# Delta rule in a hybrid decoder trunk: the order of work between the last projection and the chunk loop

## The reference

```python
p = h @ w_in                                   # q, k, v, z and two gates
qkv, z, b_pre, a_pre = split(p)
conv = silu(sum_j ext[:, j:j+L] * conv_w[j])   # four taps over time
new_conv = ext[:, L:]                          # an output: the last rows
q, k, v = split(conv); q, k = l2_normalize(q) * GD_DK**-0.5, l2_normalize(k)
def step(S, chunk):                            # one chunk, per head
    decay = exp(gam[t] - gam[s]) for s <= t
    a_mat = strict_lower(beta * (k @ k.T) * decay) + I
    u = solve(a_mat, beta * v)
    w = solve(a_mat, beta * exp(gam) * k)
    u = u - w @ S
    o = (q * exp(gam)) @ S + ((q @ k.T) * decay) @ u
    S = exp(g_last) * S + (k * exp(g_last - gam)).T @ u
o = head_rms(o) * silu(z)
y = o @ w_out
```

## Time and profile before

| | us |
|---|---|
| median of 3 runs | 2780.66 (2773.72 to 2782.38) |
| profiled execution, its own time | 2781.01 |
| its span in the profile | 2779.5 |
| PE busy | 2699.7 (97% of the span) |
| DVE busy | 1301.7 (47%) |
| ACT busy | 894.0 (32%) |
| POOL busy | 196.2 (7%) |
| chain that ended last | PE 86%, DVE 6%, ACT 3%, issue 3%, DMA 1%, POOL 1% |

### The profile page before, as it was taken

One profiled execution on the slowest core, in us unless ns is written; L12 is line 12 of the kernel. 1 busy time (PEld: TensorE's weight loads), 2 busy tenths in 40 slices (PEclk: granted clock), 3 DMA queues, 4 the chain that ended last, 5 costly groups with the idle time before them and its releaser, 6 DMA issues.

```text
span 2779.5 us, 49878 instructions
## 1 busy us (share of the span) xinstructions
PE 2699.7 (97%) x21474; PEld 2591.4 (93%) x21474; DVE 1301.7 (47%) x2086; ACT 894.0 (32%) x1127; POOL 196.2 (7%) x171
## 2 busy tenths in 40 slices
PE   7999999999989999999999999999899989999999
PEld 7999999887876999999999999999797977999998
DVE  5444334335484444433444423678435673444422
ACT  4333222134233333322222222443424342333322
POOL 2000000011010100000000000001221000100000
PEclk9999999999999999999999999999999999999999
DMA  4333324222484233332233332223215582333331
GB/s 124 91 91 102 94 77 121 54 77 68 124 270 147 77 94 94 93 105 79 81 92 91 105 94 75 63 69 90 62 43 144 170 267 87 91 91 91 105 94 52
DMA packets 476867, 280.69 MB, mean 101 GB/s; under 512 B 24940, under 2 KB 465005, under 8 KB 476707
## 3 DMA queue, kind: packets, MB, share of 16 engines
q1 hardware_dynamic: 449720, 230.83, 29.4%
q0 software_dynamic: 8704, 33.56, 3.3%
q10 hardware_dynamic: 18314, 14.45, 1.6%
HBM read 261.31 MB, written 17.69 MB: 100 GB/s over the span
## 4 chain that ended last, share of the span: by engine, by line
PE 86%; DVE 6%; issue 3%; ACT 3%; DMA 1%; POOL 1%; ACTq 0%; SPq 0%; DVEq 0%; POOLq 0%
PE ACC L436 24%; PE ACC L437 24%; PE ACC L438 24%; PE ACC L1133 2%; PE M L2219 1%; DVE w_lo L531 1%; DMA raw<-in_xa_w_k 1%; ACT w_hi L525 1%; PE ACC L2219 1%; DVE cache L1234 1%; PE M L1487 1%; DVE w_lo L546 1%; PE M L2381 1%; PE M L1562 1%; PE M L1516 1%
## 5 line engine op out<-in xcount | busy, mean ns | idle before, releaser
L436 PE MATMUL ACC<-xg_hi,w_hi 128*128 128x260 f32 x3968 | 1130.2, 285 | 11.3 <-DVE w_lo L907 7.6
L437 PE MATMUL ACC<-xg_lo,w_hi 128*128 128x260 f32 x3968 | 1124.2, 283 | 0.0
L438 PE MATMUL ACC<-xg_hi,w_lo 128*128 128x260 f32 x3968 | 1123.6, 283 | 0.0
L531 DVE TENSOR_TENSOR w_lo<-raw,w_hi 128x1024 fp32r<-128x1024 f32 (+1 forms) x326 | 421.9, 1294 | 975.9 <-ACT w_hi L525 975.6
L436 PEld LDWEIGHTS ACC<-xg_hi,w_hi 128*128 128x128 f32 x3968 | 750.5, 189 | 13.1 <-issue 8.5
L437 PEld LDWEIGHTS ACC<-xg_lo,w_hi 128*128 128x128 f32 x3968 | 751.1, 189 | 0.0
L438 PEld LDWEIGHTS ACC<-xg_hi,w_lo 128*128 128x128 f32 x3968 | 751.1, 189 | 0.0
L525 ACT ACTIVATE w_hi<-raw 128x1024 fp32r<-128x1024 f32 (+1 forms) x326 | 363.4, 1115 | 1161.8 <-PE ACC L438 1143.6
L437 PE MATMUL ACC<-hid_lo,w_hi 128*128 128x260 f32 x1408 | 399.3, 284 | 0.0
L436 PE MATMUL ACC<-hid_hi,w_hi 128*128 128x260 f32 x1408 | 398.2, 283 | 0.0
L438 PE MATMUL ACC<-hid_hi,w_lo 128*128 128x260 f32 x1408 | 398.0, 283 | 0.0
(11 more groups left out here) (556 smaller groups left out, 3262.1 us busy)
## 6 DMA issues: line engine op xcount, KB each, us to landing
raw<-in_ffn_w_gate SPq DMA_DIRECT2D x88, 512.0 KB, 3.8
raw<-in_ffn_w_up SPq DMA_DIRECT2D x88, 512.0 KB, 3.8
raw<-in_ffn_w_down SPq DMA_DIRECT2D x64, 704.0 KB, 4.6
cache<-in_cache_mem_k POOLq DMA_DIRECT2D x16, 1024.0 KB, 8.8
cache<-in_cache_mem_v POOLq DMA_DIRECT2D x16, 1024.0 KB, 8.2
raw<-in_gd_w_in SPq DMA_DIRECT2D x32, 512.0 KB, 4.2
raw<-in_ml_w_in SPq DMA_DIRECT2D x24, 512.0 KB, 3.9
raw<-in_xa_w_q SPq DMA_DIRECT2D x16, 512.0 KB, 4.4
```

Of the source, the lines that this page charges most:

```text
L436: pe.matmul(out, wh, hi[:, k0 + k, m], start=begin, stop=False)
L437: pe.matmul(out, wh, lo[:, k0 + k, m], start=False, stop=False)
L438: mm = pe.matmul(out, wl, hi[:, k0 + k, m], start=False, stop=end)
L531: dve.tensor_tensor(w_lo[:, j % 2, 0:n], raw[:, (j + d) % 4, 0:n], w_hi[:, j % 2, 0:n].bitcast(F32), ALU.subtract).then_inc(w_split, 1)
```

## The change

Six edits, all around the entry of the chunk loop:

1. The last four rounds of `substitute` and `turned` move from the end of DVE's step 7 (after the low part and the taking out of the sums) to its start.
2. `scr_w` and `scr_x` get semaphores of their own. The four transfers of chunk 0 into `XTs` start when `scr_w` has landed; POOL clears `Xs` and SP fills it when `scr_x` has. So for chunk 0 `XTs` goes first, and for the others `Xs` as before.
3. y5 waits for `Xs` alone, x5 for `XTs`. DVE's `keys(0)` waits for `scr_w` and for `turned`, no longer for `scr_x`.
4. The memory to memory copy of old convolution rows (`out_s_conv`) moves from behind the write of `scr_x` to behind the eight transfers of chunk 0.
5. ACT copies the sample keys (`sample_rows`, k8t) in step 6 of `GD_Z` rather than step 7, and applies Silu to z after `values(0)` and `conv_rows` rather than ahead of them.
6. PE waits for DVE to take out the last sums only ahead of `conv_rows`, not ahead of `values(0)` and `keys(0)`.

```diff
@@ names of ACT's events
-                       + ["z", ("v", 0)] + [("cv", n) for n in range(3)] + [(s, 0, g) for s in ("Y5", "Y6") for g in G2]
+                       + [("v", 0)] + [("cv", n) for n in range(3)] + ["z"] + [(s, 0, g) for s in ("Y5", "Y6") for g in G2]
@@ SP
-                sp.dma_start(scr_x.rearrange("c h b i j -> (c h b) i j"), blk[:]).then_inc(gd_wst, 16)
-                sp.dma_start(o["s_conv"][:, 0:2, :], a["state_gdn_conv"][0][:, 1:3, :]).then_inc(gd_st, 16)
-                sp.wait_ge(gd_wst, 32)
+                sp.dma_start(scr_x.rearrange("c h b i j -> (c h b) i j"), blk[:]).then_inc(gd_xst, 16)
+
+                def blocks(to, src, c, done):
+                    for b in range(4):
+                        r = slice(32 * b, 32 * b + 32)
+                        sp.dma_start(to[r, :, r], src[c, :, b].rearrange("h i j -> i h j")).then_inc(done, 16)
 
                 def spread(c):
                     if c == 0:
+                        sp.wait_ge(gd_wst, 16)
+                        gd_pool.wait(sp, "zt")
+                        blocks(XTs, scr_w, c, gd_xt)
+                        sp.wait_ge(gd_xst, 16)
                         gd_pool.wait(sp, "zx")
+                        blocks(Xs, scr_x, c, gd_xs)
                     else:
                         gd_dve.wait(sp, "XT5", c - 1, 1)
-                    for to, src in ((Xs, scr_x), (XTs, scr_w)):
-                        for b in range(4):
-                            r = slice(32 * b, 32 * b + 32)
-                            sp.dma_start(to[r, :, r], src[c, :, b].rearrange("h i j -> i h j")).then_inc(gd_xs, 16)
+                        blocks(Xs, scr_x, c, gd_xs)
+                        blocks(XTs, scr_w, c, gd_xt)
                 spread(0)
+                sp.dma_start(o["s_conv"][:, 0:2, :], a["state_gdn_conv"][0][:, 1:3, :]).then_inc(gd_st, 16)
                 spread(1)
@@ PE
-                    pe.wait_ge(gd_xs, 16 * 8 * (n + 1))
+                    pe.wait_ge(gd_xs, 16 * 4 * (n + 1))
                     each("y5", n, C, lambda h: rr5[:, h, :], lambda h: Xs[:, h, :])
 
                 def x5(n):
+                    pe.wait_ge(gd_xt, 16 * 4 * (n + 1))
@@ PE, entry
-                pe.wait_ge(acc_free, GD_Z.t0 + GD_Z.units)
                 gd_dve.wait(pe, "qkS")
                 gd_act.wait(pe, "k8")
                 values(0)
                 keys(0)
+                pe.wait_ge(acc_free, GD_Z.t0 + GD_Z.units)
                 conv_rows()
@@ ACT, work in the steps of GD_Z
-                z = {0: lambda: conv_silu(act, 23), 1: sample_conv, 4: sample_norms, 7: sample_rows}
+                z = {0: lambda: conv_silu(act, 23), 1: sample_conv, 4: sample_norms, 6: sample_rows}
@@ ACT, entry
+                gd_act.wait(act, "kd")
+                act.wait_ge(mm_done, GD_Z.u0 + GD_Z.units)
+                values(0)
+                conv_rows()
                 act.wait_ge(acc_free, GD_Z.t0 + GD_Z.units)
                 for n in range(4):
                     z = gp[:, 24 + 2 * n:26 + 2 * n, :]
                     ins = act.activation(z, z, ACT.Silu)
                 gd_act.done(ins, "z")
-                gd_act.wait(act, "kd")
-                values(0)
-                conv_rows()
@@ DVE, work in the steps of GD_Z
-                     5: lambda: (sample_scaled(), substitute(18, 22)), 6: lambda: (sample_dots(), substitute(22, 27)),
-                     7: lambda: (substitute(27, 31), turned())}
-                return k, q, v, z
+                     5: lambda: (sample_scaled(), substitute(18, 22)), 6: lambda: (sample_dots(), substitute(22, 27))}
+                last = {7: lambda: (substitute(27, 31), turned())}
+                return k, q, v, z, last
@@ DVE, entry
-                dve.wait_ge(gd_wst, 32)
+                dve.wait_ge(gd_wst, 16)
+                gd_dve.wait(dve, "WT")
                 keys(0)
@@ POOL
-                pool.wait_ge(gd_wst, 32)
+                pool.wait_ge(gd_xst, 16)
                 gd_pool.done(pool.memset(Xs[:], 0.0), "zx")
@@ DVE, the phase
-            dve_phase(dve, own, GD_Z, after=z)
+            dve_phase(dve, own, GD_Z, after=z, first=last)
```

More of the change, by code:

```diff
@@ L1987, in program @@
         gd_xs = sem("gd_xs")
+        gd_xt = sem("gd_xt")
+        gd_xst = sem("gd_xst")
         gd_ps = sem("gd_ps")
@@ L3137, in _ @@
                 dve_phase(dve, own, ph)
-            k, q, v, z = GDX.dve_prepare(dve, own)
+            k, q, v, z, last = GDX.dve_prepare(dve, own)
             dve_phase(dve, own, GD_K, after=k)
```

## The result

| | before | after |
|---|---|---|
| median | 2779.85 us (14 runs) | 2785.36 us (14 runs) |
| ratio, with its 95% interval | | 1.0023 (1.0014 to 1.0031) |
| the same kernel in two later sets | | 1.0015 (1.0004 to 1.0025), 1.0011 (1.0000 to 1.0021) |
| profiled execution | 2781.01 | 2788.14 |
| last unit of z to the start of xt5 of chunk 0 | 22.57 | 24.38 |

The forecast was 2779.3, a gain of 1.7. The change loses: about 2 us at the entry of the chunk loop, where all its edits are, and 3 to 6.5 us in the times. Three sets of the kernel before against itself gave 1.0000, 0.9999 and 0.9988 (the last with an interval of 0.9976 to 0.9999, which leaves out 1), so one set can be off by 0.1% and more. The lengths at the entry, read from profiles, are much firmer: 24.35, 24.69, 24.28 and 24.45 to y6 in four profiles of the kernel before, 26.38, 26.26 and 26.59 in three of the changed one.

A forecast was written before the change was run, and what follows sets the result against it. PE, busy 97% of the span, was taken as the bound, with gain only where it waits at the chunk loop's entry. y5 3.80 us earlier, limited by ACT and the clock to 1.7, gave 2781.01 to 2779.3; range 2774 to 2784.

The forecast's parts named there:

- The shares, the gaps and the chain into y5: PE busy 97%; entry gaps of 3.15, 3.41 and 5.05 us, the last ended by scr_x's write, clearing and eight transfers.
- Edits 1 to 3: At the chunk loop's entry, y5 starts 3.80 us earlier: 1.91 from the earlier rounds, 1.89 from four fewer issues ahead.
- The wait moves from the transfers to ACT: At the entry, the Silus moved behind the convolution issues are late by some 2 us, holding Yb's copy until 1974.53.
- x5 is what decides: y5 has slack behind it; x5 waits for ACT's Yb and starts at 1975.18, 2.53 us earlier.
- ACT's order (edit 5): At the entry, cvA at 1965.05, cvC at 1967.18, issues done at 1969.38, then 5.15 us of table load and Silus.
- rival B: PE's 4.2 us idle lowers the clock before conv_rows; y6 2.3 us slower, total 2783.3 us; chance 0.20.
- its own sign of being wrong: Last unit of z to xt5 (22.6 us) shorter by over 4 us or longer by over 2.5.
- the other sign: Granted clock at 0.5 from before conv_rows at the entry, which would mean the slower case of 2783.3 us.
- the values of x5 and xt5: Gain by where the clock returns: 3.40 with x5 full, 1.66 with x5 low, -0.1 with xt5 low too.
- The rule on transposes: Transposes do not count as busy like matmuls, so the entry would be cold before conv_rows; the prediction's trace spoke against it.
- The edit that I priced at nothing, edit 4: Moving out_s_conv: between minus 0.8 and plus 0.8 us on y5's start, taken as nothing because y5 has slack.
- within 0.3%: Whole kernel: median indistinguishable from no change, within about 0.3% or 8.3 us; chance 0.92.

The follow-up runs named there:

- e10: The changed kernel with the copy out_s_conv issued behind scr_x again, as before the change; 2781.71 us, ratio 1.0012.
- e1: The changed kernel with three of ACT's four Silus of z moved early into steps 5 and 6 of phase z; 2779.59 us, ratio 0.9998.
- e6: The changed kernel with ACT's four Silus back ahead of values(0) and the convolution rows; 2779.06 us, ratio 1.0004.
- before_again: The kernel before, unaltered, profiled a second time; y6 came 24.3 to 24.7 us behind the last unit, as in all four of its profiles.
- before_third: The kernel before, unaltered, profiled a third time; y6 came 24.3 to 24.7 us behind the last unit, as in all four of its profiles.
- e3: The changed kernel plus 40 useless transposes on PE in the gap ahead of the convolution rows; 2780.16 us, ratio 0.9996.
- e9: e7 plus 38 useless transposes on PE between the last convolution copy and y5; 2775.98 us, ratio 0.9994.
- e5: The kernel before with edit 1 alone (last rounds and turn ahead of the low part and sums); 2775.03 us, ratio 0.9989.
- e8: The kernel before with edits 1 and 5 only (last rounds early; sample keys in step 6, Silus behind convolution rows); 2782.99 us, ratio 1.0014.
- e2: The changed kernel with edit 1 undone, so DVE takes out the last sums ahead of the last rounds and turn; 2778.87 us, ratio 0.9994.
- after_again: The changed kernel, unaltered, with a second profile and set of times; 2784.20 us, ratio 1.0015.
- e4: The changed kernel with edit 1 undone and three Silus moved early into steps 5 and 6; 2776.56 us, ratio 0.9986.
- e7: The changed kernel with Silus early, last sums taken out between last round and turn, first convolution row not waiting for them; 2774.23 us, ratio 0.9988.

## Why the prediction was wrong

- The shares, the gaps and the chain into y5 were read rightly. Edits 1 to 3 did what they were to do: y5 started 11.5 behind the last unit, forecast 12.6. That is 1.0 better, of which 0.8 is the quicker landing of scr_x; the copy's move can be 0.2 of that (e10), the rest of it is open.
- "The wait moves from the transfers to ACT" was right, and so was that x5 is what decides. The forecast put Yb's copy at 16.7; it came at 20.1.
- **The step that failed is the start of the convolution rows in "ACT's order (edit 5)".** I priced the 24 transposes at the full clock (cvC at 9.4) although my own sum had PE idle for 4.2 us ahead of them, where it had been 3.15. That case stood as rival B, with chance 0.20, and it is what happens, in three profiles of three, and in e1, e6 and e10, which have the same gap of 4.4. I held against it that the clock had stayed full with PE idle from 1964.60 to 1968.00. One profile showed one way through the entry; before_again and before_third show the other one for the same kernel, with a gap of only 3.14 and 3.15. Of B's price, cvC at 11.6 was right (measured 11.4). That its y6 at 26.7 is so near (measured 26.3 to 26.6) is luck: it had Yb's copy at 19.0 (20.1 to 20.5), without the stalled issue, and in return xt5 at the low clock throughout (3.54), which took 1.95 to 2.17.
- By the length that the prediction set as its own sign of being wrong (over 2.5 longer to xt5; it was 1.8) it would have stood. By the other sign, the granted clock at 0.5 ahead of conv_rows, B came true, and e3 shows the failed step by itself: with the clock kept up, cvC and Yb come at the forecast 9.4 and 16.8.
- With what the Trainium skill says in "TensorE: Matmul & The Clock Gate", section "Part 1: The HAM clock gate", of turns that differ from run to run, the four profiles of the kernel before agree: two and two. I had cited it for the values of x5 and xt5, but not applied it to the rows ahead of y5.
- The rule on transposes in the Trainium skill, "TensorE: Matmul & The Clock Gate", section "Part 4: PE-mode transpose", is not borne out for the float32 transposes of this kernel: e3 (40) and e9 (38) keep the clock at full by transposes alone, and in e5 it comes back at 1963.1 after nothing but transposes. The rows name them MATMUL and do not tell whether they are of the mode that the section means.
- **The edit that I priced at nothing, edit 4, costs 1.6 on Yb's copy** (18.6 behind the last unit in e10, 20.1 to 20.5 with the edit), of which 0.6 to 0.9 reach y6. I looked for its price on SP and on y5; it fell on ACT's issues, and so on Yb.
- After both, Yb is at 20.1 and not 16.7: 2.0 from the clock, and 1.4 from the issues (the stalled one is 1.6 longer, and a pause of 0.3 ahead of the last one is gone). x5 then runs low, as forecast.
- For the whole kernel the entry explains the sign and only a part of the size: it costs 2.0 (four profiles against three), while the three sets of times say 3 to 6.5 (ratios 1.0011 to 1.0023). Self-comparisons of up to 0.12%, 3.3 us, make chance a possible part of this. The profiles show no other place: behind y6 the two kernels are alike (797.3 to 799.3 and 798.6 to 798.8), and ahead of the entry executions of the changed kernel alone differ by 8.5 us. The rest stays open. My chance of 0.92 for "within 0.3%" held; the range of 2774 to 2784 was too narrow at the top, as it took B's 2783.3 with 1 us for the spread of runs.

## What to carry to other kernels

Two edits can lose together (e8) though the one alone (e5), and the other without it (e2), do no harm. Work hidden in a wait is hidden only while it ends before that wait does; here it was moved directly ahead of what the other engine waits for, and its full length (5.15 us) stood in that wait. So where work is put behind a wait, add up when that wait ends under the low clock as well. A clock that is read from one profile of a stretch with gaps is one sample: take a second profile before a rival is given a small chance.

## What the runs showed of the hardware that I had not expected

- A transfer issue on ACT took 1.9 to 2.0 us in place of 0.3 when it began 1.6 to 1.8 us behind SP's issue of a 192 KB copy from memory to memory (after, three profiles, and e1). With the copy 6.7 us ahead of ACT's first issue (e10) or 4.7 (e6), none did. The issue outlasted the copy's traffic: in after_again DMA moved 786 GB/s over the quarter of a microsecond from 1970.75, as many bytes as the copy has, and nothing in the next one, while the issue lasted from 1970.95 to 1972.94. The mechanism stays open. Two smaller delays, 0.7 to 0.9 us, stand in e2 and in e4, where the copy is issued only after ACT's issues.
- PE's clock can be lower for longer idle and the stretch still be shorter: e5 idles 6.10 us and has the clock back for y5 and x5, while the kernel before, in the profile of the prediction idle for 3.15, then 3.41, then 5.05, runs y5 and most of x5 low.
- Filler on PE holds the clock: in e9, 38 transposes (4.37 us) in the wait, and y5 and x5 at 2.02 each in place of 3.75 and 2.96 in e7. It is worth 2.6 us from the start of y5 to y6.
- The turns of v and k right behind the last unit (1.91 us) did not put off the fall of the clock: it came 3.9 to 4.7 us behind that unit with them (after, three profiles, e1, e6, e10), and 4.2 to 4.3 behind it with PE idle (e5, e8).
